# Upper and lower activation parts in one 512-column product, in convolution's input blocks and attention's queries and keys

## What is computed

```python
def short_conv_mixer(h, w_in, conv_k, w_out):
    b, c, u = jnp.split(h @ w_in, 3, axis=-1)
    y = depthwise_causal_conv(c * u, conv_k)      # 3 taps, per feature
    return (b * y) @ w_out

def dilated_attention_mixer(h, w_qkv, w_out, rel_bias):
    q, k, v = (h @ w_qkv) split in three          # 16 heads of 64
    ... three dilated branches, softmax, weighted sum ...
    return o @ w_out

for i in range(2):
    h = rms_norm(x, mix_norm[i])
    x = x + (short_conv_mixer if i == 0 else dilated_attention_mixer)(h)
    h = rms_norm(x, ffn_norm[i])
    x = x + swiglu(h)                              # width 2816
```

## Time and profile before

| | |
|---|---|
| median of 3 runs | 955.33 us (954.2 to 958.57) |
| the profiled execution, its own time | 958.16 us |
| its span in the profile | 956.1 us |
| TensorE busy | 942.1 us, 99% |
| VectorE busy | 743.2 us, 78% |
| ScalarE busy | 540.4 us, 57% |
| granted TensorE clock, mean | 0.994 |
| convolution's input blocks on TensorE | 387.9 to 457.4 us |
| attention's rounds 0 to 3 on TensorE | 658.6 to 743.7 us |

### The profile page before, as it was taken

The page is one execution under the profiler, slowest core; times in us unless marked ns, Lnnn a source line. Parts: engine busy times, 40 slices in busy tenths (PEclk is TensorE's granted clock), DMA queues, the critical chain, the costliest instruction groups (busy, mean ns, idle before and its releaser), DMA issues.

```text
span 956.1 us, 15251 instructions
## 1 busy us (share of the span) xinstructions
PE 942.1 (99%) x6383; PEld 812.3 (85%) x6383; DVE 743.2 (78%) x841; ACT 540.4 (57%) x687; POOL 63.7 (7%) x60
## 2 busy tenths in 40 slices
PE   8999999999999999999999999999999999999997
PEld 5799888988878788999888888889999888888886
DVE  2699978878887887787669987777776668987874
ACT  3584467466546465634265664657655656655554
POOL 0000660000100000100000000010000000000000
PEclk9999979999999999999999999999999999999999
DMA  9877224766798878556536878778653464978761
GB/s 338 298 255 284 72 84 140 271 219 253 174 354 213 315 182 309 208 181 212 202 115 166 269 214 272 214 212 288 257 170 128 144 218 142 259 217 269 216 176 44
DMA packets 41555, 204.54 MB, mean 214 GB/s; under 512 B 3408, under 2 KB 5904, under 8 KB 25744
## 3 DMA queue, kind: packets, MB, share of 16 engines
q1 hardware_dynamic: 35024, 180.37, 52.0%
q0 software_dynamic: 5760, 22.05, 12.4%
q10 hardware_dynamic: 704, 1.17, 0.4%
HBM read 202.49 MB, written 1.07 MB: 213 GB/s over the span
## 4 chain that ended last, share of the span: by engine, by line
PE 88%; DVE 6%; ACT 2%; DMA 1%; issue 1%; POOL 1%; SPq 0%; DVEq 0%; POOLq 0%; ACTq 0%
PE bank L2179 44%; PE acc L2179 41%; PE bank L2830 2%; DMA X_inv<-stream 1%; DVE w_lo L1419 1%; POOL X_inv L839 1%; PE bank L2576 1%; ACT w_hi L933 0%; DVE scores L1443 0%; DVE XT L1725 0%; PE bank L2281 0%; PE acc L2281 0%; PE bank L2286 0%; PE bank L2453 0%; DVE qkT L1713 0%
## 5 line engine op out<-in xcount | busy, mean ns | idle before, releaser
L1419 DVE TENSOR_TENSOR w_lo<-raw,w_hi 128x2048 fp32r<-128x2048 f32 x125 | 284.5, 2288 | 51.0 <-ACT w_hi L933 50.7
L933 ACT ACTIVATE w_hi<-raw 128x2048 fp32r<-128x2048 f32 x125 | 237.4, 1911 | 66.1 <-PE acc L2179 41.5
L2179 PE MATMUL bank<-w_hi,h_parts 128*128 128x512 f32 x696 | 225.0, 393 | 0.0
L2179 PE MATMUL acc<-h_parts,w_hi 128*128 128x256 f32 x928 | 169.7, 285 | 1.3 <-DVE h_parts L1471 0.7
L2179 PEld LDWEIGHTS bank<-w_hi,h_parts 128*128 128x128 f32 x696 | 130.7, 188 | 29.7 <-DVE h_parts L1496 1.5
L2179 PEld LDWEIGHTS acc<-h_parts,w_hi 128*128 128x128 f32 x928 | 142.3, 188 | 5.7 <-DVE w_lo L1541 2.1
L2179 PE MATMUL bank<-w_lo,h_parts 128*128 128x512 f32 x348 | 135.6, 390 | 0.0
L2179 PE MATMUL acc<-h_parts,w_lo 128*128 128x256 f32 x464 | 130.6, 281 | 0.0
L2179 PE MATMUL acc<-w_hi,o_hi 128*128 128x512 f32 x296 | 117.3, 396 | 1.8 <-DVE w_lo L1419 1.8
L2179 PE MATMUL acc<-w_hi,o_lo 128*128 128x512 f32 x296 | 115.4, 390 | 0.0
L2179 PE MATMUL acc<-w_lo,o_hi 128*128 128x512 f32 x296 | 115.3, 390 | 0.0
(11 more groups left out here) (412 smaller groups left out, 1353.7 us busy)
## 6 DMA issues: line engine op xcount, KB each, us to landing
raw<-stream SPq DMA_DIRECT2D x141, 1024.0 KB, 5.1
t_tables<-stream SPq DMA_DIRECT2D x9, 1024.0 KB, 5.9
x_res<-stream SPq DMA_DIRECT2D x9, 1024.0 KB, 8.1
x_res<-stream POOLq DMA_DIRECT2D x9, 1024.0 KB, 8.7
t_tables<-stream POOLq DMA_DIRECT2D x9, 1024.0 KB, 10.5
raw<-stream SPq DMA_DIRECT2D x6, 512.0 KB, 10.5
AT<-stream SPq DMA_DIRECT2D x2, 1024.0 KB, 11.6
qkT<-stream SPq DMA_DIRECT2D x2, 1024.0 KB, 13.0
```

The source lines that it names most:

```text
L933: act.activation(split_tile((w_hi, w_hi2), w), split_source(w), ACT.Copy).then_inc(s.hi_ready, 1)
L1419: dve.tensor_tensor(split_tile((w_lo, w_lo2), w), split_source(w), split_tile((w_hi, w_hi2), w), ALU.subtract).then_inc(s.lo_ready, 1)
L2179: return pe.matmul(o, l, r, start=start, stop=stop, skip_group_check=True)
```

## The change

In `wide_column_block`, which takes the place of `column_block` in the convolution's input blocks and in attention's q and k, upper weights by upper and lower activations are one product of 512 columns, into two places of a PSUM bank; lower weights by upper activations stay a product of 256 columns, into the first place. So a block fills two banks, and each 256 columns of the result lie there twice, as a main sum and a lower sum. ScalarE copies the lower sums to SBUF and VectorE adds them to the main ones. In the convolution the blocks of a round come in the order c, b, u instead of b, c, u; c and u use the same two banks, one after the other, and b two others. In attention q uses banks A0 and A1, k A2 and A3, v A0 (before A2), the values A3. TensorE gets waits for the sums that must have been read. Cut to its core:

```diff
     if w not in LABEL:
-        return ROW_OF["w", FFN_ROWS[f] + 3 * JF + w - FFN_BASE[f] - len(MADE)]
+        n = w - FFN_BASE[f] - len(MADE)
+        if f == 0 and n < 12:
+            n += (1, -1, 0)[n % 3]
+        return ROW_OF["w", FFN_ROWS[f] + 3 * JF + n]
...
+        h_both = h_parts[:, H_SHIFT[0]:H_SHIFT[0] + 2 * KD * T].rearrange("p (part k t) -> p k part t", part=2, k=KD)
...
+        qk_sum_rows = cu[:, :, 2:T + 2]
...
-        conv_banks = [[b[:, :] for b in B[0:3]], A[0:3]]
+        lower_b, upper_b, lower_a, upper_a = bank[:, 0:D], bank[:, D:2 * D], acc[:, 0:D], acc[:, D:2 * D]
+        conv_banks = [(lower_b, upper_a), (upper_b, lower_a), (upper_a, lower_b), (lower_a, upper_a)]
...
@@ ScalarE @@
+            def low_copy(i, n):
+                act.wait_ge(s.block_used, STEP[CONV_BASE + 3 * i + n])
+                if n == 1 and i:
+                    act.wait_ge(s.by_ready, i)
+                elif n != 1 and i + n:
+                    act.wait_ge(s.cu_ready, 2 * i + n // 2)
+                act.activation(two(gated if n == 1 else right), parts_of(conv_banks[i][n % 2])[1], ACT.Copy).then_inc(s.bank_copied, 1)
...
                 if i == 0:
                     hi(w + 3)
+                    low_copy(0, 0)
                     row_copy(2)
-                hi(w + 4)
+                    hi(w + 4)
+                else:
+                    low_copy(i, 0)
                 hi(w + 5)
+                low_copy(i, 1)
                 hi(w + 6)
+                low_copy(i, 2)
+                if i < 3:
+                    hi(w + 7)
                 act.wait_ge(s.by_ready, i + 1)
                 act.activation(o_hi[:, 2 * i:2 * i + 2, :], yb, ACT.Copy).then_inc(s.by_hi, 1)
...
+            def qk_low_copy(i, n):
+                act.wait_ge(s.block_used, STEP[QKV_BASE + 3 * i + n])
+                if i + n:
+                    act.wait_ge(s.qk_scaled, 3 * i + 2 * n)
+                act.activation(qk_sum_rows, parts_of((lower_a, upper_a)[n])[1], ACT.Copy).then_inc(s.bank_copied, 1)
...
                 if i == 0:
                     hi(w + 3)
+                    qk_low_copy(i, 0)
                     row_copy(4)
                 if i < 4:
                     hi(w + 4)
...
                 if i < 4:
+                    if i:
+                        qk_low_copy(i, 0)
                     hi(w + 5)
+                    qk_low_copy(i, 1)
                     hi(w + 6)
@@ VectorE @@
+                taken, gating = (parts_of(banks)[0] for banks in conv_banks[i])
                 if i == 0:
                     lo(w + 2)
                     lo(w + 3)
+                dve.wait_ge(s.block_used, STEP[w])
+                dve.wait_ge(s.bank_copied, 4 + 3 * i + 1)
+                dve.tensor_tensor(two(c_sb), taken, inputs, ALU.add).then_inc(s.cu_ready, 1)
+                if i == 0:
                     dve.wait_ge(s.row_copied, 1)
                     link(dve.tensor_tensor(rrow2[:, :], rrow[:, :], rrow[:, :], ALU.mult))
-                lo(w + 4)
+                dve.wait_ge(s.cu_ready, 2 * i + 1)
+                link(dve.tensor_tensor(two(c_sb), two(c_sb), both(rrow2[:, :]), ALU.mult))
+                if i == 0:
+                    lo(w + 4)
+                lo(w + 5)
                 dve.wait_ge(s.block_used, STEP[w + 1])
-                link(dve.tensor_tensor(two(c_sb), two(conv_banks[i % 2][1]), both(rrow2[:, :]), ALU.mult))
-                lo(w + 5)
+                dve.wait_ge(s.bank_copied, 4 + 3 * i + 2)
+                link(dve.tensor_tensor(gates, gating, gates, ALU.add))
+                link(dve.tensor_tensor(gates, gates, both(rrow[:, :]), ALU.mult))
+                if i < 3:
+                    lo(w + 6)
                 dve.wait_ge(s.block_used, STEP[w + 2])
+                dve.wait_ge(s.bank_copied, 4 + 3 * i + 3)
+                link(dve.tensor_tensor(inputs, taken, inputs, ALU.add))
                 cu_in = cu[:, :, 2:T + 2]
-                dve.tensor_tensor(cu_in, two(c_sb), two(conv_banks[i % 2][2]), ALU.mult).then_inc(s.cu_ready, 1)
+                dve.tensor_tensor(cu_in, two(c_sb), inputs, ALU.mult).then_inc(s.cu_ready, 1)
...
-                link(dve.tensor_tensor(yb, yb, two(conv_banks[i % 2][0]), ALU.mult))
-                dve.tensor_tensor(yb, yb, both(rrow[:, :]), ALU.mult).then_inc(s.by_ready, 1)
-                lo(w + 6)
+                dve.tensor_tensor(yb, yb, gates, ALU.mult).then_inc(s.by_ready, 1)
+                lo(w + 6 if i == 3 else w + 7)
...
+            def qk_sum(i, n):
+                dve.wait_ge(s.bank_copied, 16 + 2 * i + n + 1)
+                link(dve.tensor_tensor(qk_sum_rows, parts_of((lower_a, upper_a)[n])[0], qk_sum_rows, ALU.add))
...
                     lo(w + 4)
-                    dve.wait_ge(s.block_used, STEP[w])
+                    qk_sum(i, 0)
...
-                    dve.wait_ge(s.block_used, STEP[w + 1])
-                    dve.tensor_tensor(k2[:, i % 2, :, :], two(A[1]), both(rrow[:, :]), ALU.mult).then_inc(s.qk_scaled, 1)
+                    qk_sum(i, 1)
+                    dve.tensor_tensor(k2[:, i % 2, :, :], qk_sum_rows, both(rrow[:, :]), ALU.mult).then_inc(s.qk_scaled, 1)
@@ TensorE @@
+            def wide_column_block(w, banks, n=None, halfway=None, between=None, ahead=2):
...
+                    mm(banks[:, 512 * mt:512 * mt + 512], wh[:, k, c], h_both[:, k, :, :], k == 0, False)
+                    ins = mm(banks[:, 512 * mt:512 * mt + 256], wl[:, k, c], h_hi[:, k, :], False, k == KD - 1)
+                ins.then_inc(s.block_used, 1)
...
+                taken, gates = conv_banks[i]
+                if i == 1:
+                    pe.wait_ge(s.row_copied, 1)
                 if i >= 2:
                     pe.wait_ge(s.by_ready, i - 1)
-                column_block(w, conv_banks[i % 2][0], ...)
-                column_block(w + 1, conv_banks[i % 2][1], ...)
-                column_block(w + 2, conv_banks[i % 2][2])
+                wide_column_block(w, taken, ...)
+                if i >= 2:
+                    pe.wait_ge(s.cu_ready, (2, 6)[i - 2])
+                wide_column_block(w + 1, gates, ...)
+                pe.wait_ge(s.cu_ready, 2 * i + 1)
+                wide_column_block(w + 2, taken)
...
                 if i < 4:
-                    column_block(w, A[0], ...)
-                    column_block(w + 1, A[1], ...)
-                    pe.wait_ge(s.lo_ready, w + 3)
                     if i:
                         pe.wait_ge(s.v_scaled, TT * i)
+                    wide_column_block(w, lower_a, ...)
+                    if i >= 2:
+                        pe.wait_ge(s.pv_lo, i + 1)
+                    wide_column_block(w + 1, upper_a, ...)
+                    pe.wait_ge(s.lo_ready, w + 3)
+                    pe.wait_ge(s.qk_scaled, 3 * i + 2)
...
                     if i < 4:
+                        pe.wait_ge(s.qk_scaled, 3 * i + 3)
                         values(a, Bs, pT2, dil_v(b), out=A[3])
```

More of the change, by code:

```diff
@@ L583, in build @@
         A = [acc[:, 512 * i:512 * (i + 1)] for i in range(4)]
-        B = [ctx.enter_context(nc.psum_tensor(f"bank{i}", [P, 512], F32)) for i in range(4, 8)]
+        bank = ctx.enter_context(nc.psum_tensor("bank", [P, 2048], F32))
+        B = [bank[:, 512 * i:512 * (i + 1)] for i in range(4)]
         STAT = B[2]
@@ L587, in build @@
         minus_sinks = [A[1][:, 384:400], A[3][:, 384:400]]
-        conv_banks = [[b[:, :] for b in B[0:3]], A[0:3]]
-        Bs = [b[:, :] for b in B]
+        Bs = B
+        lower_b, upper_b, lower_a, upper_a = bank[:, 0:D], bank[:, D:2 * D], acc[:, 0:D], acc[:, D:2 * D]
+        conv_banks = [(lower_b, upper_a), (upper_b, lower_a), (upper_a, lower_b), (lower_a, upper_a)]
         acc_of = [None, A, Bs, A, A, A]
@@ L599, in halves, with parts_of @@
             return v[:, :, 0], v[:, :, 1]
+        def parts_of(banks):
+            v = banks.rearrange("p (mt part t) -> p part mt t", mt=2, part=2)
+            return v[:, 0], v[:, 1]
         def second_by_offset(ap, l):
@@ L2059, in _ @@
             dve.wait_ge(s.pool_zeroed, 6)
+            gates, inputs = two(gated), two(right)
             for i in range(4):
                 w = CONV_BASE + 3 * i
+                taken, gating = (parts_of(banks)[0] for banks in conv_banks[i])
                 if i == 0:
@@ L2228, in column_block @@
                                 k == 0 and mt == 0, k == KD - 1)
+                ins.then_inc(s.block_used, 1)
+            def wide_column_block(w, banks, n=None, halfway=None, between=None, ahead=2):
+                pe.wait_ge(s.lo_ready, w + 1)
+                wh, wl = high_of(w), low_of(w)
+                order = [(k, mt) for k in range(KD) for mt in range(2)] if n is not None else \
+                    [(k, mt) for mt in range(2) for k in range(KD)]
+                for k, mt in order:
+                    if n is not None and mt == 0:
+                        if k == ahead and between is not None:
+                            between()
```

(31 more changed lines are left out.)

10 lines of the change are left out of this document (5 added, 5 removed).

## The result

| | before | after |
|---|---|---|
| median | 954.11 us | 963.27 us |
| lowest to highest of six runs | 953.36 to 958.57 | 960.09 to 965.39 |
| ratio | | 1.0093 [1.0078, 1.0107] |
| the profiled execution, own time | 958.16 | 963.42 |
| its span, mean granted clock | 956.1, 0.994 | 961.6, 0.994 |

The change makes the kernel 9.2 us slower, by more than the 0.5% that a measurement can tell. The median lies 0.2 us inside the upper end of the range (963.5), 3.7 us above the predicted 959.6.

A forecast was written before the change was run, and what follows sets the result against it. TensorE, busy 99% and one unbroken chain in rounds of both stages, was taken as the bound. Convolution -0.3 and attention +4.6 us gave +4.3 us, from a median of 955.33 to 959.6 us; 8-in-10 range 955.8 to 963.5.

The forecast's parts named there:

- places and sizes of the waits: TensorE waits before v of attention's rounds 0 (3.5 us) and 3 (2.3 us), and u of the convolution's round 1 (1.6 us).
- the added work is hidden: Convolution and attention: ScalarE's copies (12 us) and VectorE's sums and waits (14 us) cost nothing where nobody waits.
- the saving: Convolution and attention blocks: one 512-column product for two of 256 saves 10.3 ns, 3.3 us over 320 pairs.
- Waits as worked out, clock steady: Convolution and attention: the waits come as computed without a clock fall, 959.6 us; chance 0.46.
- The clock falls in the wait: Rival: TensorE's clock halves in one of the waits, 3 us at the lower level, 1.5 us lost, 961.1 us; chance 0.34.
- My upper bound: Clock rival's price in the waits: at most 6 us, half of the 12 us between the earlier trace's clock rows.
- clock fallen for longer: One of two reasons given for the range's upper end, 963.5 us; the other is engines further behind.

## Why the prediction was right, and where it was not

**Right: places and sizes of the waits.** Forecast 3.5, 2.3 and 1.6 us, with 0.1 in round 2 and none in round 1; measured by starts 3.5, 2.2 and 1.5, no other over 0.3. The releasers are those named: q's scaling, the sum of c. It came from following each engine's list from one row to the next, and from counting the wait in full, since the stages of before were one unbroken piece of TensorE. The first of the three, gone with its fall of the clock (and with a shorter wait in round 3), was worth 4.8 us.

**Right: the added work is hidden.** Copies measured 0.58 to 0.60, sums 0.68 us; the version whose largest wait of TensorE in these stages is 0.2 us carries all 20 of each and is 1.3 us faster than before.

**Wrong size: the saving.** "One of 512 in place of two of 256 saves 237.4 - 227.1 = 10.3 ns", "320 x 10.3 ns = 3.3 us". Measured 5 ns, 1.6 us, by the blocks (5.70 against 5.62); the medians of the two kernels that differ only in the merging agree (1.7 us). I took the 227.1 ns from other blocks, in which the weights move, and added it to the 118.7; here the two take 351 and not 345.8 ns. Why is open: order and the two places of the source are ruled out, and with the activations at offset 0 six blocks take 346.7 ns, so the sum that I made does hold at another placement. The Trainium skill, TensorE: Matmul & The Clock Gate, Part 1, has a fixed cost of about 2.5 ns for a product, by which, as an estimate, the saving would have been 0.8 us; the measurement lies between that and mine, nearer to the page's. This term is off by 1.7 us.

**Wrong case: the clock.** "Waits as worked out, clock steady: 0.46" was the likeliest, on the ground that the trace of before shows one fall only, behind several us of small products and not behind one gap. But in these stages that trace has no wait of TensorE over 0.3 us, so it could say nothing against the fall. The rival "The clock falls in the wait" (0.34) is what happened, and twice in the profiled execution: behind the waits of 3.4 and 2.0 us. One execution of six, 960.09 us, was by its clock the likeliest case after all. The price of the rival was too low as well: "3 us at the lower level, 1.5 us lost", where v ran 5.5 and 3.4 us at that level, which cost 2.5 and 1.5 us. The reason that I gave for the lower end, that v feeds TensorE densely at once, did not shorten it: v kept TensorE busy for 2.00 of 2 us at 674 to 676, with the clock at 0.50. My upper bound, 6 us from the earlier trace rows, held both together. This case is off by 4.0 us.

The forecast had waits of 3.5 + 2.3 + 1.6 + 0.1 = 7.5 us (with 0.1 of round 2 and the rounding in it), no clock and a saving of 3.3: +4.3. Measured 7.2, 4.0 and 1.6: +9.6, where the medians differ by 9.2. Two errors of one sign, 5.7 us, and the range held only because it had been stretched for "clock fallen for longer". Even so there is luck in it: the forecast stood on a before of 955.33 us, where six runs give 954.11. As a difference the upper end of the range was +8.2 us, and the change measured +9.2.

**Not explained.** The convolution grew by 0.9 us, where a wait of 1.5 less 12 x 0.08 = 1.0 is 0.5. Of the other 0.4 the starts show 0.1 in the first distance behind the wait (414.10 to 414.44 instead of 0.23 us) and 0.25 at the last input block, whose first product starts 0.26 us behind the one before it and 0.34 us ahead of the next (447.77, 448.03, 448.37). What held it there isn't shown.

## What to carry to other kernels

Where TensorE is one unbroken chain, an edit that shares a buffer between it and an engine that reads it must be costed by the reader's list: what stands ahead of the read there (a `lo` of 2.3 us, 3.5 us of exponentials) is the wait, and moving the read ahead of it is worth far more than the product saved. Add to a standstill of about 2 us or more what the clock takes behind it in most executions, here 1.5 to 2.5 us, nearly the wait once again. Don't take a product's price from other blocks to the nanosecond: 5 ns of 232 halved this change's gain, and the place of the activations alone moved a pair by nearly as much. And read distances block by block: a mean over blocks of two speeds shows neither.

## What the runs showed of the hardware

- **A standstill costs twice.** In the profiled executions, waits of 1.2, 1.25 and 1.3 us left the granted clock at 1.00; those of 2.0, 2.2 and 3.4 us were each followed by a fall to 0.50, which cost 1.5, 1.55 and 2.5 us. Nothing was measured between 1.3 and 2.0 us. In one of six executions of the kernel after, by its mean clock of 0.999, neither wait was followed by such a fall.
- **Products of zeros hold the clock.** Fourteen 512-column products of a zero tile in the first wait of attention and eight in the second kept it at 1.00, and the stage was 4.1 us shorter.
- **A 512-column float32r product isn't one price.** 227 ns in the output blocks, with the weights moving; 231 to 232.5 in the input blocks, with the activations moving, whether the 256s stand between them or behind them and whether the columns come from one place or two.
- **Placement moves it, in two steps.** With the activations at column 0 or 64 of their buffer a pair of 512 and 256 takes 346.7 ns in some blocks and 353 in the others of the same execution, at column 32 always 351.
